# Seven half-size products for eight in the last seven groups of the gate projection, with the scan blocks on a twelve-half grid

## The chip, the cores and the metric

One NeuronCore of one Trainium2 chip runs the whole program. The metric is the device time of one execution in microseconds (us); the time of the kernel before is the median of three executions. TensorE is called PE below, VectorE DVE, ScalarE ACT, GpSimd POOL, and SyncE SP.

## What is computed

One decoder layer is computed for 576 tokens (512 of a prompt and 64 new ones) of width 2048. Cut to what matters here:

```
proj = einsum('bld,dn->bln', x, w_in)               # x: tokens x 2048, w_in: 2048 x 10240
u_a, z_a, b_c, c_c, h_c, z_c, g_a, g_c = split(proj) # widths 6 x 1024, then 2 x 2048
...
h  = associative_scan(lam, B u_a)                    # complex diagonal state, 64 groups of 16 channels
y_a = gelu(Re(C h) + d * u_a); y_a = y_a * sigmoid(y_a @ w_glu)
y_a = (y_a * silu(z_a)) @ w_out_a
y_c = (b_c * conv3(c_c * h_c) * silu(z_c)) @ w_out_c
merged = sigmoid(g_a) * y_a + sigmoid(g_c) * y_c
out = layernorm(2**0.25 * x + merged @ w_o)
```

All of it is in float32. The two gates g_c and g_a, 4096 outputs of width, are where the change is made: a plain product of a 4096 x 2048 weight with the 2048 x 576 tokens, followed by a sigmoid.

## The kernel before

**Halves.** All dense products are cut into halves. A half is one weight tile of 1024 inputs by 128 outputs (512 KB); it is loaded by SP into one of three buffers `w_raw`, and split by ACT into a rounded part `w_hi` and by DVE into the rest `w_lo`, since PE multiplies in a format that keeps only part of a float32. Tokens are split in the same way (`xh`, `xl`). For each of the 8 blocks of 128 inputs PE then does three products (hi with hi, hi with lo, lo with hi), each on two sets of 288 tokens: 48 matmuls of 288 columns in a half. In the last stage, the output projection, tokens are taken 288 at a time, and a half there has 24 matmuls.

**Order.** The program is written out by hand, engine by engine, as a loop over h, the number of the half. Halves 0 to 15 make u, 16 to 79 the four inputs of the convolution, 80 to 95 z_a (`H_ZA`), 96 to 159 the gates (`H_G`), 160 to 167 the GLU (`H_GLU`), then 16 halves for each of the two output products, and 64 short ones for the last. In step h of its loop ACT and DVE make the split of half h + 2 (`split(h + 2)`). ACT's part waits until half h - 1 is done, since buffers go round by three. What takes the accumulators of half h waits for `half_done` of h, so it stands at the end of step h.

**The scan.** It is cut into 8 blocks of 8 groups. Every step of a block has a place in the loop over h: `ssm_step(h, off)` gives b when h = 16 + SSM_PER * b + off. `SSM_PER` is 16. A block takes: loads of its matrices and of u by POOL (`load_mats`, `load_u`), DVE's tables and matrices, at off 7 a first product on PE (`states_in`, with `taps`), DVE's scan, swaps of halves through POOL's DMA queue, at off 19 the second product on PE (`outputs`), and last gelu and a store to `y_dram`. DVE and ACT do these in `scan_steps(h)`, which stands at the end of step h, behind what waits for half h.

**Around the GLU.** The GLU needs y, eight pieces of 128 x 576, read back from `y_dram` into two buffers `y_in`, and split by ACT (`y_high`) and DVE (`yl`). This was done one piece in each of the steps 152 to 159, `Y_LOAD` to `Y_LOAD` + 8. The GLU's steps on ACT and DVE also wait for `sz_in` and `gc_in`, which SP loads once the last sigmoid is stored.

Of the kernel before, what the change touches and what calls it, by code (L numbers as in the profile page):

```python
# [10 lines left out]
P = 128  # L11
# [23 lines left out]
NG = 8  # L35
NW = 3
# [16 lines left out]
H_GLU = H_G + 4 * KX  # L53
# [3 lines left out]
O_PER = 2 * KX  # L57
H_END = H_O + 2 * O_PER


SSM0 = H_CONV
SSM_PER = 16
Y_LOAD = SSM0 + SSM_PER * (BLK - 1) + 23

# [11 lines left out]
def ssm_step(h, off):  # L76

    b, r = divmod(h - off - SSM0, SSM_PER)
    return b if r == 0 and 0 <= b < BLK else None

# [14 lines left out]
def build(nc, d):  # L95
# [80 lines left out]
    st = u_raw  # L176
# [17 lines left out]

    r = Region(s0)
    yh = r("yh", [P, NB, TOK], F32R)
    yl = r("yl", [P, NB, TOK], F32R)
    y_in = [r(f"y_in{i}", [P, TOK]) for i in range(2)]
    r2 = r.at
    merged = r("merged", [P, KX, TOK])  # L200
    r = Region(x0)
    gch = r("gch", [P, NB, TOK], F32R)
    gcl = r("gcl", [P, NB, TOK], F32R)
    gah = r("gah", [P, NB, TOK], F32R)
    gal = r("gal", [P, NB, TOK], F32R)
    assert r.at <= s0
# [7 lines left out]
    mh = nc.alloc_sbuf_tensor_at("mh", [P, KX, TOK], F32R, offset=x0)  # L214
    ml = nc.alloc_sbuf_tensor_at("ml", [P, KX, TOK], F32R, offset=s0)


    r = Region(x0 + 4 * KX * TOK)
    r_all = r("r_all", [P, KX, TOK])
    assert r.at <= s0  # L220
# [155 lines left out]
    norm_ready = sem("norm_ready")  # L376
    out_ready = sem("out_ready")
# [12 lines left out]
    def _(sp):  # L390

        def load_half(h):
            if h >= H_END:
                return
            if h >= NW:
                sp.wait_ge(lo_ready, h - NW + 1)
            sp.dma_start(w_raw[:, h % NW, :], d["w"][h if h < H_O + O_PER else h - O_PER]).then_inc(raw_loaded[h % NW], 16)

# [33 lines left out]
        for h in range(H_CONV, H_GLU):  # L432
# [11 lines left out]
            if Y_LOAD <= h < Y_LOAD + NB:  # L444
                n = h - Y_LOAD
                if n == 0:
                    sp.wait_ge(y_made, BLK)
                    sp.wait_ge(y_stored, U_LOAD * (BLK - 1))
                if n == NB - 1:
                    sp.wait_ge(y_stored, U_LOAD * BLK)  # L450
                if n >= 2:
                    sp.wait_ge(yl_ready, n - 1)
                sp.dma_start(y_in[n % 2][:, :], y_dram[n]).then_inc(y_loaded[n % 2], 16)
        store_out(NB + 2 * KX - 1, g_sig, 2 * KX, sg_dram[2 * KX - 1])
# [24 lines left out]
        for s in range(4):  # L479
            sp.wait_ge(out_stored[s], 16 * (NB + 2 * KX) // 4)  # L480
        for n in range(2):
            load_sz(n)
            load_gc(n)
# [47 lines left out]
    def _(pool):  # L531
# [21 lines left out]
        def load_u(b):  # L553
            for s in range(2):
                pool.wait_ge(u_stored[s], 16 * (b + 2 - s) // 2 if b < NB - 1 else 16 * NB // 2)
            if b:
                pool.wait_ge(hl_ready, b)
# [30 lines left out]
        def scan_moves(h):  # L588
            if (b := ssm_step(h, -1)) is not None:
                load_mats(b)  # L590
            if (b := ssm_step(h, 2)) is not None:
                load_u(b)
# [3 lines left out]
            if (b := ssm_step(h, 12)) is not None:  # L596
                pool.wait_ge(s_ready, b + 1)
                swap(v_sw, v_st, s_swapped)
            if (b := ssm_step(h, 11)) is not None:
                store_k(b)  # L600
            if (b := ssm_step(h, 13)) is not None:
                load_lt(b)
            if (b := ssm_step(h, 25)) is not None:
                store_y(b)

        store_mq()
        for h in range(SSM0 - 1, SSM0 + SSM_PER * (BLK - 1) + 26):
            scan_moves(h)

    @blk.tensor  # L610
    def _(pe):
# [83 lines left out]
        for h in range(H_CONV, H_GLU):  # L695
# [3 lines left out]
            if (b := ssm_step(h, 19)) is not None:  # L699
                outputs(b)  # L700
# [3 lines left out]
            half(h, par, xh, xl, h % 2 * KH, h % 2 == 0, h % 2 == 1)  # L704
        for h in range(H_GLU, H_O):
# [35 lines left out]
        for h in range(H_O, H_END):  # L741
            t, u = divmod(h - H_O, O_PER)
            if u % 4 < 2:
                fresh(h % 2)
# [6 lines left out]
            half(h, h % 2, mh, ml, (u // 2) % 2 * KH, u % 4 < 2, u % 4 >= 2,  # L751
# [4 lines left out]
    def _(act):  # L756

        def split(h):
            if h >= H_END:
                return  # L760
            act.wait_ge(raw_loaded[h % NW], 16 * (h // NW + 1))
            if h >= NW:
                act.wait_ge(half_done, h - NW + 1)
            act.activation(w_hi[h % NW][:, :], w_raw[:, h % NW, :], ACT.Copy).then_inc(hi_ready, 1)  # L764
# [15 lines left out]
        def scan_steps(h):  # L780
            if (b := ssm_step(h, 19)) is not None:
# [5 lines left out]
            if (b := ssm_step(h, 4)) is not None:  # L787
# [5 lines left out]
            if (b := ssm_step(h, 5)) is not None:  # L793
                act.wait_ge(lb_ready, b + 1)
                act.activation(lbh[:, :, :], mb[:, :, :, :].rearrange("p g c s -> p g (c s)"), ACT.Copy)\
                   .then_inc(lbh_ready, 1)
                act.wait_ge(u_loaded, U_LOAD * (b + 1))
# [13 lines left out]
            if (b := ssm_step(h, 10)) is not None:  # L811
# [4 lines left out]
            if (b := ssm_step(h, 15)) is not None:  # L816
# [4 lines left out]
            if (b := ssm_step(h, 22)) is not None:  # L821
# [24 lines left out]
        for h in range(H_CONV, H_ZA):  # L846
            split(h + 2)
            n, l = divmod(h - H_CONV, 8)
# [14 lines left out]
            scan_steps(h)  # L863

        for h in range(H_ZA, H_G):
            split(h + 2)
            if h % 2:
# [5 lines left out]
            scan_steps(h)  # L873
# [5 lines left out]
        for h in range(H_G, H_GLU):  # L879
            split(h + 2)  # L880
            if Y_LOAD < h <= Y_LOAD + NB:
                y_high(h - Y_LOAD - 1)
            if h % 2:
                n = (h - H_G) // 2
                act.wait_ge(half_done, h + 1)
                act.wait_ge(out_stored[n % 4], 16 * ((n + NB) // 4))
# [3 lines left out]
            scan_steps(h)  # L890
# [77 lines left out]
    def _(dve):  # L968
# [6 lines left out]
        def split(h):  # L975
            if h >= H_END:
                return
            dve.wait_ge(hi_ready, h + 1)
            dve.tensor_tensor(w_lo[h % NW][:, :], w_raw[:, h % NW, :], w_hi[h % NW][:, :].bitcast(F32),  # L979
                              ALU.subtract).then_inc(lo_ready, 1)  # L980

# [177 lines left out]
        def turn_table(b):  # L1159
# [452 lines left out]
```

## Time and profile before

| | |
|---|---|
| Median of 3 executions | 1577.58 us (1576.66 to 1577.72) |
| Profiled execution, its own time | 1577.16 us |
| Its span, first to last instruction | 1575.3 us |
| Granted TensorE clock, mean | 0.995 |
| PE busy | 1545.9 us, 98% |
| DVE / ACT / POOL busy | 830.0 / 444.3 / 189.0 us |

The span is what the rows count from. 1.9 us of the execution's time lie outside it. Busy is the union of an engine's instructions; a matmul's recorded length (297 ns) overlaps with the next, so PE's pace is read from starts or from counted pieces of the chain, not from that length.

### The profile page before, as it was taken

The page shows a single profiled execution, that of the slowest core. Times are in us where ns is not written, and L with a number is a line of the kernel's source. Part 1 is how long each engine was busy: PE and PEld are TensorE (multiplying, and loading weights), DVE is VectorE, ACT ScalarE, POOL GpSimd, SP SyncE. Part 2 cuts the span into 40 slices and gives each one's busy share as a digit, 9 for nine tenths or more (in the row PEclk, how much of TensorE's full clock was granted, in tenths as well). Part 3 has the DMA queues.
Part 4 walks back from the last instruction along what each step waited for, and adds up shares of the span by engine and source line. Part 5 has one row for each costly group of instructions (what it writes and reads, how often), then busy time and mean ns, then how long its engine had stood idle before and what let it go on. Part 6 is the DMA issues. An engine that isn't in the chain of part 4 may idle for free.

```text
span 1575.3 us, 26995 instructions
## 1 busy us (share of the span) xinstructions
PE 1545.9 (98%) x11690; PEld 1539.2 (98%) x11690; DVE 830.0 (53%) x1177; ACT 444.3 (28%) x582; POOL 189.0 (12%) x348
## 2 busy tenths in 40 slices
PE   8999999999999999999999999999999999999994
PEld 8999999999999999999999999999999999999994
DVE  5977374464463553643633533223733355666887
ACT  4222222222122122222222222133411122333444
POOL 0110040230311311302204113010000000000000
PEclk9999999999999999999999999999999999999997
DMA  9352362452543543634625535344544443555573
GB/s 304 125 152 91 92 166 79 116 158 75 133 133 94 146 117 122 176 109 132 161 83 165 136 115 147 104 156 150 189 141 134 125 127 125 160 187 183 183 221 107
DMA packets 87447, 221.21 MB, mean 140 GB/s; under 512 B 19744, under 2 KB 28576, under 8 KB 87328
## 3 DMA queue, kind: packets, MB, share of 16 engines
q1 hardware_dynamic: 71456, 188.78, 38.6%
q0 software_dynamic: 15872, 30.70, 8.6%
q8 instruction: 92, 1.51, 0.4%
q14 instruction: 27, 0.22, 0.0%
HBM read 186.55 MB, written 28.16 MB: 136 GB/s over the span
## 4 chain that ended last, share of the span: by engine, by line
PE 94%; DVE 3%; SPq 1%; DMA 1%; issue 1%; ACT 0%; DVEq 0%
PE acc L634 91%; SPq L420 1%; DMA w_raw<-in_w 1%; PE s_ps L656 1%; DVE r_all L1495 0%; PE s_ps L680 0%; PE s_ps L682 0%; DVE w_lo L979 0%; DVE r_all L1494 0%; PE s_ps L657 0%; PE s_ps L681 0%; PE s_ps L679 0%; PE k_ps L666 0%; DVE rstd L1488 0%; DVE r_all L1460 0%
## 5 line engine op out<-in xcount | busy, mean ns | idle before, releaser
L634 PE MATMUL acc<-xh,w_hi 128*128 128x288 f32 x2560 | 550.9, 297 | 3.9 <-DVE xl L987 3.7
L634 PE MATMUL acc<-xh,w_lo 128*128 128x288 f32 x2560 | 549.5, 296 | 0.0
L634 PE MATMUL acc<-xl,w_hi 128*128 128x288 f32 x2560 | 549.2, 296 | 0.0
L979 DVE TENSOR_TENSOR w_lo<-w_raw,w_hi 128x1024 fp32r<-128x1024 f32 x263 | 321.8, 1224 | 406.8 <-ACT w_hi L764 405.1
L764 ACT ACTIVATE w_hi<-w_raw 128x1024 fp32r<-128x1024 f32 x263 | 278.0, 1058 | 597.3 <-PE acc L634 578.2
L634 PEld LDWEIGHTS acc<-xh,w_hi 128*128 128x128 f32 x2560 | 412.9, 189 | 6.4 <-DVE w_lo L997 2.3
L634 PEld LDWEIGHTS acc<-xh,w_lo 128*128 128x128 f32 x2560 | 413.4, 188 | 0.0
L634 PEld LDWEIGHTS acc<-xl,w_hi 128*128 128x128 f32 x2560 | 413.4, 188 | 0.0
L634 PE MATMUL acc<-mh,w_hi 128*128 128x288 f32 x512 | 152.2, 297 | 1.0 <-DVEq L983 0.7
L634 PE MATMUL acc<-ml,w_hi 128*128 128x288 f32 x512 | 151.3, 296 | 0.0
L634 PE MATMUL acc<-mh,w_lo 128*128 128x288 f32 x512 | 151.3, 296 | 0.0
L634 PEld LDWEIGHTS acc<-mh,w_hi 128*128 128x128 f32 x512 | 96.1, 188 | 1.7 <-DVEq L983 0.9
L634 PEld LDWEIGHTS acc<-ml,w_hi 128*128 128x128 f32 x512 | 96.1, 188 | 0.2
L634 PEld LDWEIGHTS acc<-mh,w_lo 128*128 128x128 f32 x512 | 96.1, 188 | 0.0
L887 ACT ACTIVATE out_st<-acc 128x576 f32<-128x576 f32 x32 | 20.9, 654 | 189.6 <-PE acc L634 189.6
L564 POOL DMA_DIRECT2D v_sw<-v_st x32 | 18.3, 577 | 446.4 <-DVE v_st L1204 417.7
L634 PE MATMUL acc<-gcl,w_hi 128*128 128x288 f32 x256 | 55.0, 296 | 0.0
L634 PE MATMUL acc<-gch,w_lo 128*128 128x288 f32 x256 | 55.0, 296 | 0.0
L634 PE MATMUL acc<-gal,w_hi 128*128 128x288 f32 x256 | 55.0, 296 | 0.0
L634 PE MATMUL acc<-gah,w_hi 128*128 128x288 f32 x256 | 55.0, 296 | 0.0
L634 PE MATMUL acc<-gah,w_lo 128*128 128x288 f32 x256 | 54.9, 296 | 0.0
L634 PE MATMUL acc<-gch,w_hi 128*128 128x288 f32 x256 | 54.9, 296 | 0.0
(275 smaller groups left out, 1467.1 us busy)
## 6 DMA issues: line engine op xcount, KB each, us to landing
w_raw<-in_w SPq DMA_DIRECT2D x263, 512.0 KB, 3.8
sg_dram<-out_st SPq DMA_DIRECT2D x32, 288.0 KB, 4.6
v_sw<-v_st POOLq DMA_DIRECT2D x32, 144.0 KB, 3.9
gc_in<-sg_dram SPq DMA_DIRECT2D x16, 288.0 KB, 2.7
sz_in<-sg_dram SPq DMA_DIRECT2D x16, 288.0 KB, 2.7
x_in<-in_xT SPq DMA_DIRECT2D x32, 144.0 KB, 2.2
outT<-o_st SPq DMA_DIRECT2D x32, 144.0 KB, 1.8
mb<-mq_dram POOLq DMA_DIRECT2D x8, 512.0 KB, 6.6
```

Of the source, the lines that this page charges most:

```text
L420: sp.dma_start(k_dram[part, b, :, :, 0:KROW - T * GC].rearrange("x p n -> p x n"), zeros[:, :, :]).then_inc(zeros_stored, 16)
L564: pool.dma_start(to[64 * x:64 * x + 64, :, :], of[64 - 64 * x:128 - 64 * x, :, :]).then_inc(done, 16)
L634: ins = pe.matmul(acc[:, par, t, 0:TH], w, m[:, k0 + k, t * TH:(t + 1) * TH], start=first and k == 0 and n == 0, stop=last and k == KH - 1 ...
L656: pe.matmul(out_of(g), lbh[:, g, :], u, start=True, stop=False)
L764: act.activation(w_hi[h % NW][:, :], w_raw[:, h % NW, :], ACT.Copy).then_inc(hi_ready, 1)
L887: act.activation(two(out_st[n % 4][:, :]), halves_of(acc[:, n % 2]), ACT.Sigmoid).then_inc(g_sig, 1)
L979: dve.tensor_tensor(w_lo[h % NW][:, :], w_raw[:, h % NW, :], w_hi[h % NW][:, :].bitcast(F32), ALU.subtract).then_inc(lo_ready, 1)
```

## The change

Three things are changed together.

1. The last seven of the sixteen groups of four halves in the gates (28 halves) are done as seven products for eight. Such a group is two output tiles (of 128) times two input halves (of 1024): weights A11, A12, A21, A22, and tokens in two input halves and two sets of 288. In Winograd's form of Strassen's scheme seven products of 24 matmuls replace eight. The weights of four of them (S1 to S4) are sums, made by DVE in place (`weight_sums`). The tokens of four of them are sums too (`token_sums`, once, in the eight steps before). DVE adds the products up in pieces of 128 x 288 (`keep`, `out_st`), and ACT applies the sigmoid to the finished tile. The 49 units count as halves 132 to 180, so `H_GLU` is 181.
2. `SSM_PER` is 12. The blocks' steps are moved together (`outputs` from 19 to 16, the scan from 11 to 10, the swaps back from 12 to 11), `load_mats` and `load_u` of the next block come right behind the first swap, the scan's result `st` lies in `v_sw`, no longer in `u_raw`, and `scan_steps(h)` stands directly behind `split(h + 2)` in all stages.
3. The pieces of y are loaded and split in steps 175 to 180, the last six units.

```diff
-SSM_PER = 16
-Y_LOAD = SSM0 + SSM_PER * (BLK - 1) + 23
+SSM_PER = 12
+KINDS = ("A11", "A12", "S2", "S1", "S3", "S4", "A22")
+UNIT_AT = {(kind, n): H_S + 7 * n + i for n in range(NSG) for i, kind in enumerate(KINDS)}
+X_SUMS = H_S - 9
+Y_LOAD = UNIT_AT["A11", NSG - 1]
+Y_STEP = (1, 2, 3, 4, 5, 5, 6, 6)
...
+        def load_y(n):
+            if n < 2:
+                sp.wait_ge(y_stored, U_LOAD * BLK)
+                sp.wait_ge(lo_ready, UNIT_AT["S3", NSG - 2] + 1)
+            else:
+                sp.wait_ge(yl_ready, n - 1)
+            sp.dma_start(y_in[n % 2][:, :], y_dram[n]).then_inc(y_loaded[n % 2], 16)
...
+        def product(h, ps, m):
+            (mh_, ml_), k0, t = m
+            pe.wait_ge(lo_ready, h + 1)
+            for k in range(KH):
...
+                for i, (w, x) in enumerate(((wh, mh_), (wh, ml_), (wl, mh_))):
+                    ins = pe.matmul(ps, w, of_half(x[:, k0 + k, :], t), start=k == 0 and i == 0,
...
+        def weight_sums(h):
+            for kind, of, to in (("S3", "A11", "A21"), ("S2", "S3", "A22"), ("S1", "A21", "A22"), ("S4", "S2", "A12")):
...
+                dve.wait_ge(lo_ready, h + 3)
+                if kind in ("S3", "S2"):
+                    dve.wait_ge(group_loaded[to, n % 2], 16 * (n // 2 + 1))
+                dve.tensor_tensor(raw_of(kind, n), raw_of(of, n), raw_of(to, n), ALU.add).then_inc(weight_sum, 1)
+                dve.wait_ge(weight_sum, sum_count(kind, n))
...
         for h in range(H_CONV, H_ZA):
             split(h + 2)
+            scan_steps(h)
...
-            scan_steps(h)
...
+        for h in range(H_S, H_GLU):
+            split(h + 2)
+            weight_sums(h)
...
+            if kind == "S4":
+                dve.tensor_tensor(of_half(o1, 1), k_f, ps, ALU.add).then_inc(c12_ready, 1)
+            if kind == "A22":
+                dve.tensor_tensor(of_half(o2, 0), k_s, ps, ALU.add).then_inc(c21_ready, 1)
...
+            for i, step in enumerate(Y_STEP):
+                if h == Y_LOAD + step:
+                    dve.wait_ge(yh_ready, i + 1)
+                    dve.tensor_tensor(yl[:, i, :], y_in[i % 2][:, :], yh[:, i, :].bitcast(F32), ALU.subtract)\
+                       .then_inc(yl_ready, 1)
```

On PE the place is half 132, the first of the 49. Before, a half goes over both token sets with each weight:

```order
L634 MATMUL acc<-xh,w_hi 128x288 x2
L634 MATMUL acc<-xl,w_hi 128x288 x2
L634 MATMUL acc<-xh,w_lo 128x288 x2
L634 MATMUL acc<-xh,w_hi 128x288 x2
L634 MATMUL acc<-xl,w_hi 128x288 x2
```

And now (`s_ps` is the scan's accumulator, used here for three of the products):

```order
L747 MATMUL acc<-xl,w_hi 128x288 x2
L747 MATMUL acc<-xh,w_lo 128x288 x2
L827 MATMUL s_ps<-xh,w_hi 128x288
L827 MATMUL s_ps<-xl,w_hi 128x288
L827 MATMUL s_ps<-xh,w_lo 128x288
```

Each weight is now used for one token set, so consecutive matmuls go to one place of the accumulator, where before they went to two in turn.

On DVE the place is the end of the gates, just ahead of the GLU (`yl` are the pieces of y, `gcl` the first of the GLU's own work). Before:

```order
L979 TENSOR_TENSOR w_lo<-w_raw,w_hi 128x1024
L1403 TENSOR_TENSOR yl<-y_in_115,yh 128x576
L979 TENSOR_TENSOR w_lo<-w_raw,w_hi 128x1024
L1403 TENSOR_TENSOR yl<-y_in_116,yh 128x576
L979 TENSOR_TENSOR w_lo<-w_raw,w_hi 128x1024
L1410 TENSOR_TENSOR gcl<-gc_in_125,gch 128x576
```

And now, from the sixth of the last seven units on:

```order
L1174 TENSOR_TENSOR w_lo<-w_raw,w_hi 128x1024
L1669 TENSOR_TENSOR out_st_94<-keep_127,acc 128x288
L1678 TENSOR_TENSOR yl<-y_in_121,yh 128x576
L1678 TENSOR_TENSOR yl<-y_in_122,yh 128x576
L1174 TENSOR_TENSOR w_lo<-w_raw,w_hi 128x1024
L1671 TENSOR_TENSOR out_st_95<-keep_125,acc 128x288
L1678 TENSOR_TENSOR yl<-y_in_121,yh 128x576
L1678 TENSOR_TENSOR yl<-y_in_122,yh 128x576
L1174 TENSOR_TENSOR w_lo<-w_raw,w_hi 128x1024
```

The last four pieces of y stand between and behind the last two sums into `out_st`, two to a unit.

On POOL one block's round of DMAs was, before:

```order
L564 DMA v_sw<-v_st 64x576 x2
L586 DMA y_dram<-y_pre 16x8x72 x8
L568 DMA k_dram<-k_hi 128x2x128
L570 DMA k_dram<-k_lo 128x2x128
L564 DMA v_sw<-v_st 64x576 x2
L580 DMA lth<-k_dram 16x8x128 x8
L580 DMA ltl<-k_dram 16x8x128 x8
L548 DMA mb<-mq_dram 128x1x1024
L549 DMA bc<-in_bC 128x1x1024
L550 DMA c_blk<-in_c_blk 128x256
L551 DMA b_blk<-in_b_blk 128x256
L560 DMA u_raw<-u_dram 16x8x72 x8
```

And now:

```order
L679 DMA v_sw<-v_st 64x576 x2
L663 DMA mb<-mq_dram 128x1x1024
L664 DMA bc<-in_bC 128x1x1024
L665 DMA c_blk<-in_c_blk 128x256
L666 DMA b_blk<-in_b_blk 128x256
L675 DMA u_raw<-u_dram 16x8x72 x8
L683 DMA k_dram<-k_hi 128x2x128
L685 DMA k_dram<-k_lo 128x2x128
L679 DMA v_sw<-v_st 64x576 x2
L695 DMA lth<-k_dram 16x8x128 x8
L695 DMA ltl<-k_dram 16x8x128 x8
L701 DMA y_dram<-y_pre 16x8x72 x8
```

The next block's twelve loads moved ahead of the second swap and of `lth`, and the store of y moved behind them.

## Rows read from the trace of the kernel before

**Rows 1.** The page: busy time, share and instructions of each engine.

```profile
PE 1545.9 (98%) x11690; PEld 1539.2 (98%) x11690; DVE 830.0 (53%) x1177; ACT 444.3 (28%) x582; POOL 189.0 (12%) x348
```

**Rows 2.** The chain in time: start us, us, what.

```profile
923.93 76.99 PE acc L634 x576
1004.45 352.03 PE acc L634 x2640
1356.96 96.00 PE acc L634 x720
```

**Rows 3.** Timeline of PE at three `states_in`: start us, us, what.

```profile
484.34 0.43 PE L634 MATMUL acc<-xh,w_lo 128*128 128x288 f32 x2
485.04 0.31 PE L656 MATMUL s_ps<-u,lbh 128*128 128x144 f32 x1 [0.27 <-issue]
...
593.32 0.43 PE L634 MATMUL acc<-xh,w_lo 128*128 128x288 f32 x2
594.78 0.30 PE L656 MATMUL s_ps<-u,lbh 128*128 128x144 f32 x1 [1.03 <-DVE lbl L1260]
...
703.06 0.43 PE L634 MATMUL acc<-xh,w_lo 128*128 128x288 f32 x2
703.64 0.30 PE L656 MATMUL s_ps<-u,lbh 128*128 128x144 f32 x1 [0.16 <-issue]
```

**Rows 4.** Timeline of DVE ahead of the first of these.

```profile
479.31 1.23 DVE L1254 TENSOR_TENSOR lcl<-lc,lch 128x1024 fp32r<-128x1024 f32 x1
...
481.91 1.22 DVE L979 TENSOR_TENSOR w_lo<-w_raw,w_hi 128x1024 fp32r<-128x1024 f32 x1
483.05 1.22 DVE L1260 TENSOR_TENSOR lbl<-mb,lbh 128x1024 fp32r<-128x1024 f32 x1
484.18 0.75 DVE L1263 TENSOR_TENSOR u<-u_raw,u 128x576 fp32r<-128x576 f32 x1
```

**Rows 5.** Timeline of DVE, three instructions of `turn_table`.

```profile
440.04 1.13 DVE L1167 TENSOR_TENSOR scr<-coarse,fine 128x512 f32<-128x512 f32 x1
441.09 1.12 DVE L1168 TENSOR_TENSOR scr<-coarse,fine 128x512 f32<-128x512 f32 x1
442.24 0.69 DVE L1169 TENSOR_TENSOR cos<-scr,scr 128x512 f32<-128x512 f32 x1
```

**Rows 6.** Groups by line: count | busy us, mean ns | idle before.

```profile
L979 DVE TENSOR_TENSOR w_lo<-w_raw,w_hi 128x1024 fp32r<-128x1024 f32 x263 | 321.8, 1224 | 406.8 <-ACT w_hi L764 405.1
L764 ACT ACTIVATE w_hi<-w_raw 128x1024 fp32r<-128x1024 f32 x263 | 278.0, 1058 | 597.3 <-PE acc L634 578.2 <-DMA w_raw<-in_w 13.1 <-ACT out_st L887 3.3
L1175 DVE TENSOR_TENSOR scr<-mb,bc 128x1024 f32<-128x1024 f32 x8 | 9.8, 1219 | 0.0
L1452 DVE SCALAR_TENSOR_TENSOR r_all<-x_in,acc 128x288 f32<-128x288 f32 x32 | 14.4, 451 | 15.0 <-PE acc L634 15.0
L1403 DVE TENSOR_TENSOR yl<-y_in,yh 128x576 fp32r<-128x576 f32 x8 | 6.0, 752 | 0.0
L877 ACT ACTIVATE yh<-y_in 128x576 fp32r<-128x576 f32 x8 | 5.4, 670 | 0.0
```

**Rows 7.** Timeline of ACT: a split after a wait for PE, and the GLU's start.

```profile
1385.86 1.06 ACT L764 ACTIVATE w_hi<-w_raw 128x1024 fp32r<-128x1024 f32 x1 [0.24 <-PE acc L634]
...
1087.72 0.65 ACT L887 ACTIVATE out_st<-acc 128x576 f32<-128x576 f32 x1 [4.70 <-PE acc L634]
1094.45 0.69 ACT L894 ACTIVATE gch<-gc_in 128x576 fp32r<-128x576 f32 x1 [4.84 <-DMA gc_in<-yc_dram]
```

**Rows 8.** SP's loads of `y_in`, from their source line.

```profile
DMA to landing us min/median/max: 2.8/4.1/5.5
```

**Rows 9.** Timeline of POOL over one block's loads of `lth` and `ltl`.

```profile
526.30 1.35 POOL L564 DMA_DIRECT2D v_sw<-v_st  x2 [3.60 <-DVE v_st L1218]
544.12 0.62 POOL L548 DMA_DIRECT2D mb<-mq_dram  x1
```

**Rows 10.** Window of first block: us, busy of PE, PEld, DVE, ACT, POOL, clock, DMA.

```profile
158.17:267.08 108.91, 108.64 (x835) 108.16 (x833) 57.76 (x73) 25.64 (x36) 19.01 (x34) 1.00 0.40 113
```

More of the change, by code:

```diff
@@ L79, in ssm_step, with unit_of, sum_count, raw_count @@
     return b if r == 0 and 0 <= b < BLK else None
+def unit_of(h):
+    return KINDS[(h - H_S) % 7], (h - H_S) // 7
+SUM_STEP = {"S3": -2, "S2": -1, "S1": 0, "S4": 1}
+def sum_count(kind, n):
+    return sum(1 for k, at in SUM_STEP.items() for v in range(NSG)
+               if 7 * v + at < 7 * n + SUM_STEP[kind]) + 1
+def raw_count(h):
+    return sum(1 for g in range(h % NW, h + 1, NW) if not H_S <= g < H_GLU)
 class Steps:
@@ L376, in build @@
     norm_ready = sem("norm_ready")
+    xs_loaded = [sem(f"xs_loaded{i}") for i in range(2)]
+    xs_sums = sem("xs_sums")
+    xs_high = sem("xs_high")
+    xs_low = sem("xs_low")
+    group_loaded = {(kind, p): sem(f"group_{kind}_{p}") for kind in ("A11", "A12", "A21", "A22") for p in range(2)}
+    weight_sum = sem("weight_sum")
+    s_kept = sem("s_kept")
+    e_ready = sem("e_ready")
+    f_ready = sem("f_ready")
+    g_ready = sem("g_ready")
+    c11_ready = sem("c11_ready")
+    c12_ready = sem("c12_ready")
+    c21_ready = sem("c21_ready")
+    c22_ready = sem("c22_ready")
     out_ready = sem("out_ready")
@@ L889, in _ @@
                 act.sem_inc(acc_free[n % 2], 1)
-            scan_steps(h)
+            if X_SUMS <= h < X_SUMS + KH:
+                j = h - X_SUMS
+                act.wait_ge(y_done, BLK)
+                act.wait_ge(xs_sums, j + 1)
+                for i in range(2):
+                    act.activation(x2h[:, j + i * KH, :], x_st[j % 2][:, i, :], ACT.Copy).then_inc(xs_high, 1)
+        first = 2 * (KX - NSG)
+        for h in range(H_S, H_GLU):
+            split(h + 2)
+            kind, n = unit_of(h)
+            m = first + 2 * n
+            if kind == "A11":
+                act.wait_ge(half_done, h + 1)
+                if n:
+                    act.wait_ge(c21_ready, n)
+                act.activation(keep[0][:, :], s_ps[:, 0, 0:TH], ACT.Copy).then_inc(s_kept, 1)
+            if kind == "S4":
+                act.wait_ge(c11_ready, n + 1)
+                act.wait_ge(c12_ready, n + 1)
+                act.activation(out_st[m % 4][:, :], out_st[m % 4][:, :], ACT.Sigmoid).then_inc(g_sig, 1)
+            if kind == "A22":
+                act.wait_ge(c22_ready, n + 1)
+                act.wait_ge(c21_ready, n + 1)
+                act.activation(out_st[(m + 1) % 4][:, :], out_st[(m + 1) % 4][:, :], ACT.Sigmoid).then_inc(g_sig, 1)
+            for i, step in enumerate(Y_STEP):
+                if h == Y_LOAD + step:
+                    act.wait_ge(half_done, Y_LOAD + 1)
+                    y_high(i)
         def gc_high(n):
@@ L1165, in turn_table @@
             s = [x[:, 0:NG * CP].rearrange("p (g a r) -> p g a r", g=NG, r=T) for x in scr]
[L1166 to L1169 removed]
+            if b:
+                dve.wait_ge(st_ready, b)
+            if part:
+                dve.wait_ge(lc_ready, b + 1)
+            out, a, op = ((cos, (k[0], k[1]), ALU.subtract), (sins, (ks[1], ks[0]), ALU.add))[part]
+            own.mark(dve.tensor_tensor(s[0], a[0], f[0], ALU.mult))
+            link(dve.tensor_tensor(s[1], a[1], f[1], ALU.mult))
+            link(dve.tensor_tensor(grid(out), s[0], s[1], op))
         def input_matrix(b):
```

311 lines of the change are left out of this document (228 added, 83 removed).

## Prediction

> **What bounds the kernel now.** I read the page first. PE is busy for 1545.9 of 1575.3 us and the next engine, DVE, for 830.0 [rows 1]. The chain in order of time then shows whether PE is really paced by its own matmuls: a run of 2640 matmuls takes 352.03 us with nothing between them [rows 2], 0.1333 us each. So a half of 48 takes 6.40 us, and whatever lies beside PE costs nothing until it delays a matmul. The same pace holds for 576 in 76.99 us, and for 720 in 96.00 us in the last stage, where halves have 24 matmuls and take 3.20 us [rows 2].
>
> Where PE waits inside the program, the timeline of PE shows it at `states_in` [rows 3]. The last matmul before it starts at 484.47 (the second of the pair at 484.34), the next at 485.04. One step of 0.13 is normal, so 0.43 us are lost. In the same way 1.19 us are lost at 594.78 and 0.32 at 703.64. In the trace the first of the eight blocks loses nothing, three lose 0.43, one 1.19 and three 0.32: 3.5 us. These, the start and the end are all that PE gives away, so the change is worth what it takes from PE's instructions, less new waits.
>
> **Fewer matmuls.** 28 halves of 48 go (1344), 49 products of 24 come (1176). 168 matmuls less, at 0.1333 us: 22.4 us. This asks that a matmul that writes where the one before wrote keeps its pace. The last stage has that pattern today, and has the pace [rows 2]. **-22.4.**
>
> **The waits at `states_in`.** What is late there today is the low part of u: the instruction that makes it ends at 484.18 + 0.75 = 484.93, and PE starts 0.11 us later [rows 3, 4]. Ahead of it on DVE stand `lcl`, two gelu instructions (the row of the first is left out; together 1.5 us), the split and `lbl` [rows 4]. In the new order the gelu has another step (off 19, not 6), and DVE no longer takes what waits for the end of the half before the scan. ACT's split begins at best 0.26 us into a half, or 1.03 us if a sigmoid or copy of 0.65 [rows 7] stands before it, and DVE's follows when that is done, 1.06 and a hand-over of 0.03 later [rows 5, 6]: at 2.12 at worst. Then `w_lo`, `lcl` and `lbl` follow at 1.14 us each (483.05 - 481.91) and u at 0.75 [rows 4]: done at 6.29, PE ready at 6.40, just when the half ends. Bounds: nothing gained, or all 3.5. I take 3.2, since each step has its row. **-3.2.**
>
> **The groups of seven.** PE takes 7 x 3.20 = 22.4 us for a group. DVE has 7 splits of 1.22, 4 weight sums (nearest row: `tensor_tensor` of 128x1024 in float32, 1.22) and 7 sums of 128x288 (0.45) [rows 6], 16.6 us; ACT 7 of 1.06, two sigmoids of 0.65 [rows 7] and a copy, 9.2 us. Neither is the bound by its sum. But they hand work to each other in order, and the tightest stretch is this: ACT's split of the next group's A11 may start when S3 is done on PE, 16.0 us into the group, and the low part of the next S1 is needed at 22.4 + 9.6 = 32.0. Between lie 0.26 for the start [rows 7], 4 high splits (4.24), 4 low (4.88), the sums for S3, S2 and S1 (3.66), the sums into `out_st` of S4 and A22 (0.90) and their sigmoids (1.30), since each step here waits for the one before: 15.24. Some 14 hand-overs of about 0.03 (442.24 - 441.09 - 1.12) [rows 5] make it 15.7. 0.3 us are left, of which PE's own 0.11 goes. So I expect no real wait, and put 0.5 for all six passages; none at the low end. At the high end hand-overs of 0.1 and small sums that take 0.65 give 17.0, 1.0 us a group, 6 us. **+0.5.**
>
> Here a page speaks. In rows 5 DVE's second instruction starts 1.05 us after the first, which is 1.13 long, and the third, which waits for a semaphore of the second, 1.15 after one of 1.12. A wait on itself costs 0.10 us, and six of them are in the stretch above (counted in it, as full lengths). The Trainium skill, "VectorE: DVE Perf Modes", section "The DRAIN you can't avoid", says that a semaphore between two such instructions "costs nothing extra here"; by it the stretch would be 15.1. The trace does not agree, and the sum goes by the trace.
>
> **The eight steps before them** add to DVE, each, 4 instructions of 0.45 and 2 of 0.75 [rows 6]: 3.3 us beside a split of 1.22 in 6.40. DVE waits there for ACT's high parts, which in odd steps stand behind a sigmoid at the end of the half, so DVE runs some 3.6 us late. A split is made two halves ahead and ends 2.6 us into its half, so 10 us of lateness hide. The first four weight tiles are loaded late (behind the last pair of tokens), 2 to 3 us past their time; same cover. **0**, up to 3 if the loads crowd.
>
> **The pieces of y.** Before, each had a half to itself. Now eight share six units of 3.20 us, with two buffers, so a piece's load can't start before the low part of the piece two before is made. A load takes 2.8 to 5.5 us, 4.1 in the middle [rows 8], the split 0.67 and 0.75 [rows 6]. I follow the last group from its start, at 4.1: the low part of piece 0 at 11.8, which makes DVE's split for S3 0.2 late (13.0 for 12.8), **+0.4** with PE's start; piece 1 at 14.3, piece 2 loaded at 16.0, made at 17.5; then A22's split, two sums and piece 3 at 20.8; piece 5 loaded at 24.9, made at 26.4. Behind it ACT and DVE do the split for half 182, the last sum (28.4) and the sigmoid (29.1), and only then piece 6 (30.6) and 7 (32.0). The GLU's first half starts at 22.65 and needs piece k 0.80 k later: piece 6 at 27.45, so PE waits 3.2, and for piece 7 0.6 more: 3.8. With loads of 2.8 the same walk leaves 1.0. The loads of weights around them are few then, so I take a value between. **+2.5.**
>
> The last sigmoid also ends about 6 us into the GLU, where it ended 0.85 in before; `gch` came 6.1 us behind it [rows 7], then some 6 us of chain to the split of the GLU's fourth half: about 19, needed at 21.7. This is covered, with 2.5 us to spare.
>
> **The twelve-half grid** takes nothing from PE: the same 8 blocks. What could cost is an engine that no longer keeps up. From the first `states_in` to the second DVE is busy for 57.8 of 108.9 us [rows 10], of which 16 splits are 19.5. A block will last 12 halves and its own 6.1 us on PE (108.9 less 16 times 6.40 and the wait of 0.43), some 83 us. If all of DVE's other 38.3 us stay, and the earlier block's gelu and y sums (3 us) come on top, that is 56 with 12 splits: two thirds. A step of the scan may end a half late on DVE without a cost, by the 10 us above. **0.**
>
> **Sum**, against the profiled execution's 1577.16: -22.4 -3.2 +0.5 +0.4 +2.5 = -22.2, **1555.0 us**. That execution is 0.4 under the median 1577.58, which is nothing here.
>
> **Rivals.** *The groups are paced by DVE and ACT.* For it: 0.3 us of slack in a stretch of 16. Against: the rows add up to less. At 1 to 3 us a group over six or seven, 1561 to 1575. Chance 0.12.
>
> *POOL's queue paces the scan (ends on the slower side).* A block has 42 DMAs there, and `lth` now stands behind twelve loads of the next block, which the order shows. At today's pace, 18 DMAs from 526.30 to 544.12 [rows 9], 0.99 us each, a round takes 42 of some 83 us; the first swap can go 4.1 us into off 8, the twelve loads are issued by 5 us into off 10, and `ltl` is issued about the end of off 13 and landed some 5 us into off 14, over a half before `outputs` at off 16, 8 us early. To lose what is gained, each of 8 `outputs` must wait 2.8 us, so POOL must be 11 us later over those 30 DMAs: 1.35 us each in place of 0.99. From there on the change is slower: at 1.6, 18 us late, 10 us a block, 1635 us. Idle for "issue" in the same bursts is up to 3 us at a time, so a crowded queue is possible. Chance 0.04.
>
> *The change doesn't do what it says, or gives it back*: the pause at the GLU lets TensorE's clock fall, or the y chain loads at 5.5 us and repeats. A few us more, 1560 to 1566 within the first case's upper end; matmuls at a slower pace in `s_ps`, no gain, 1577. Chance 0.03.
>
> **The numbers.** Forecast as above 0.81, its own range from all low ends (no wait in the groups, 1.0 for y, all 3.5 back: 1552) to 6 for the groups, 3.8 for y and 1 at the entry (1563). The range 1551.5 to 1563 leaves out about 2 in 10. Within 0.2% (3 us), about what a measurement of this kernel can tell from no change, I put 0.02; slower 0.04; faster 0.94.
>
> **What would show it.** Right: some 168 fewer matmuls, products of 3.20 us through the seven groups, `states_in` at most 0.1 us behind, and one gap of 1 to 4 us in the first half of the GLU before the seventh block. Wrong: gaps of PE before the matmuls of S1 or S3 in each group (released by `w_lo`); PE idle before `outputs` released by `lth`; a granted clock below 1.00 behind the GLU's gap.

## The result, and the profile after

The changed kernel takes 1561.04 us in the median of four executions (1557.92 to 1562.55), the kernel before 1577.65 us on the same chip (1576.66 to 1578.08): a ratio of 0.9892, 95% interval [0.9879, 0.9904]. That is 16.6 us faster, 6 us less than forecast and inside the range. The profiled execution took 1557.92 us, the fastest of the four, with a span of 1556.1. Of the runs below, one execution of grid (5157 us) and two of all4 (2401 and 2990 us) took far longer than every other; they are left out of all medians and ratios, and no trace shows why.

The page, busy time of each engine (answers to rows 1):

```profile
PE 1524.7 (98%) x11522; PEld 1518.4 (98%) x11522; DVE 935.0 (60%) x1323; ACT 475.9 (31%) x626; POOL 187.5 (12%) x348
```

PE has 168 matmuls fewer and is still busy for 98%. DVE went from 830.0 to 935.0 us, which nothing on PE feels by itself. The timeline of PE at one `states_in` (answers to rows 3: start us, us, what):

```profile
489.36 0.43 PE L747 MATMUL acc<-xh,w_lo 128*128 128x288 f32 x2
489.63 0.23 PE L769 MATMUL s_ps<-u,lbh 128*128 128x144 f32 x1
```

And DVE ahead of it (answers to rows 4):

```profile
484.58 1.23 DVE L1174 TENSOR_TENSOR w_lo<-w_raw,w_hi 128x1024 fp32r<-128x1024 f32 x1 [0.40 <-ACT w_hi L926]
485.72 1.22 DVE L1471 TENSOR_TENSOR lcl<-lc,lch 128x1024 fp32r<-128x1024 f32 x1
486.86 1.22 DVE L1477 TENSOR_TENSOR lbl<-mb,lbh 128x1024 fp32r<-128x1024 f32 x1
487.99 0.75 DVE L1480 TENSOR_TENSOR u<-u_raw,u 128x576 fp32r<-128x576 f32 x1
```

The low part of u ends at 488.74, 0.89 us before PE wants it, and PE goes on in step. All eight `states_in` are so: the whole 3.5 us came back.

What PE gives away now stands in the chain in order of time (answers to rows 2):

```profile
1064.14 0.70 ACT out_st L1080
1064.85 5.74 DMA sg_dram<-out_st
1071.11 3.06 DMA gc_in<-yc_dram
1074.25 0.68 ACT gch L1088
1074.93 0.55 ACT sig_t L1099
1075.56 38.66 PE acc L747 x288
1114.23 2.58 issue
1116.80 206.57 PE acc L747 x1536
1323.39 0.77 DVE sz_in L1717
1324.26 13.05 PE acc L747 x96
```

Read it from the top: the last sigmoid of the gates, the landing of its store, the load of `gc_in` that SP issues behind it, `gch`, and only then the sigmoid that frees PE's accumulator. From pitch to pitch PE loses 1.22 us at 1075.56 (third half of the GLU), 2.74 at 1116.80 (`H_OUTC`) and 1.07 at 1324.26 (`H_O`). Behind the second comes one cost more, seen in windows (us, busy of PE, PEld, DVE, ACT, POOL, clock, DMA):

```profile
1116.00:1118.00 2.00, 1.20 (x9) 1.23 (x10) 1.97 (x4) 0.00 (x0) 0.00 (x0) 1.00 0.11 29
1118.00:1121.30 3.30, 3.30 (x16) 3.30 (x16) 2.32 (x4) 1.63 (x2) 0.00 (x0) 0.52 0.96 327
1121.30:1124.00 2.70, 2.70 (x22) 2.70 (x21) 0.58 (x1) 0.00 (x0) 0.00 (x0) 0.95 0.63 198
```

The granted clock is 0.52 for 3.3 us, the lower level of 1.2 GHz, and 13 matmuls have a pitch of 0.240 us for 0.133: 1.4 us. So 1577.2 - 22.4 - 3.5 + 1.2 + 2.7 + 1.1 + 1.4 = 1557.7, against 1557.92 measured. That closes this execution. It leaves open why the other three took 1559.9 to 1562.6; no trace of them was kept, and the experiments show what such executions can lose.

### The profile page after: what moved, and what is told of

Same layout as the page of the kernel before. It is cut to its first block and busy times, and to the rows that moved or that the text cites. A ratio compares the mean times of both kernels' runs of the same rounds, so it can differ in the third digit from the quotient of the medians.

```text
span 1556.1 us, 27026 instructions
## 1 busy us (share of the span) xinstructions
PE 1524.7 (98%) x11522; PEld 1518.4 (98%) x11522; DVE 935.0 (60%) x1323; ACT 475.9 (31%) x626; POOL 187.5 (12%) x348
## 5 line engine op out<-in xcount | busy, mean ns | idle before, releaser
L1174 DVE TENSOR_TENSOR w_lo<-w_raw,w_hi 128x1024 fp32r<-128x1024 f32 x251 | 307.1, 1224 | 307.1 <-ACT w_hi L926 304.1
L747 PE MATMUL acc<-xh,w_hi 128*128 128x288 f32 x2112 | 455.0, 297 | 3.8 <-DVE xl L1194 3.5
L747 PE MATMUL acc<-xh,w_lo 128*128 128x288 f32 x2112 | 453.2, 296 | 0.0
L747 PE MATMUL acc<-xl,w_hi 128*128 128x288 f32 x2112 | 453.1, 296 | 0.0
L926 ACT ACTIVATE w_hi<-w_raw 128x1024 fp32r<-128x1024 f32 x251 | 264.6, 1055 | 565.5 <-PE acc L747 537.6
L747 PEld LDWEIGHTS acc<-xh,w_hi 128*128 128x128 f32 x2112 | 340.6, 189 | 6.1 <-DVE w_lo L1204 2.2
L747 PEld LDWEIGHTS acc<-xh,w_lo 128*128 128x128 f32 x2112 | 341.0, 188 | 0.0
L747 PEld LDWEIGHTS acc<-xl,w_hi 128*128 128x128 f32 x2112 | 341.0, 188 | 0.0
L1174 DVE TENSOR_TENSOR w_lo<-s_raw,w_hi 128x1024 fp32r<-128x1024 f32 x33 | 40.4, 1223 | 17.4 <-ACT w_hi L926 17.2
```

The source lines that it names most:

```text
L747: ins = pe.matmul(acc[:, par, t, 0:TH], w, m[:, k0 + k, t * TH:(t + 1) * TH], start=first and k == 0 and n == 0, stop=last and k == KH - 1 ...
L926: act.activation(w_hi[h % NW][:, :], raw, ACT.Copy).then_inc(hi_ready, 1)
L1174: dve.tensor_tensor(w_lo[h % NW][:, :], raw, w_hi[h % NW][:, :].bitcast(F32), ALU.subtract).then_inc(lo_ready, 1)
```

## The experiments

The sums of waits below are read from the pitch of PE's matmuls, less the normal step; the matmuls at a slow pace are summed in the same way (2.3 us of these are in every trace, before included). Kernels of one batch ran on one chip, beside executions of the kernel before: the first four (again to slack) beside a median of 1577.69 us, the next four (upool to all4) beside 1577.43, the last three beside 1578.09. A ratio of a run is to this median of its own batch, with its 95% interval.

**again.** The changed kernel, not edited.

> The changed kernel as it is, once more. Its four times so far lie 4.6 us apart (1557.92 to 1562.55), those of before 1.4. Theory A (the loss lies at the start of the GLU, in a load of gc_in and sz_in that waits for the store of the last sigmoid, and varies with how long that store takes): a new profile has its waits of PE at the same places, the GLU's third half, the start of the first output product and the start of the last stage, but with other lengths, 5 to 10 us in all; the rest of the span agrees within 0.3 us. Theory B (the spread is the clock's or the machine's, spread over the program): the same waits with the same lengths, and the difference somewhere else.

Measured: 1567.18 us in the median of six (1563.38 to 1571.59), ratio 0.9931 [0.9916, 0.9947]. The interval doesn't meet the first one, 0.9879 to 0.9904, though it is the same program. The profile (1566.35 us) says why, in its waits of PE (waited for: us in total, times, longest us):

```profile
PE s_ps L792 <- DMA ltl<-k_dram: 3.8, 3, 1.5
...
PE acc L747 <- issue: 2.6, 1, 2.6
...
PE acc L747 <- ACTq L1101: 1.3, 1, 1.3
```

The first row is not in the first profile at all. `outputs` waited for the landing of `ltl` in three of eight blocks (1.42, 1.20 and 1.68 us from pitch to pitch), and matmuls at a slow pace came to 7.0 us. Neither theory had this: the loss is at a new place, not at the start of the GLU. In the first profile `lth` and `ltl` had landed 3.3 to 4.7 us before `outputs` in seven blocks; in the kernel before it was 17 to 23. The last block has 9.9. The change had used up most of this cover, and whether the rest was enough differed from one execution to the next. One program can thus come out 6 us apart in two batches, so small differences between batches are judged by the waits in the traces below.

**early.** SP loads `sz` and `gc` ahead of the last two stores of `sg`.

```diff
+            if h == H_GLU - 1:
...
+                for m in range(2):
+                    load_sz(m)
+                    load_gc(m)
             if kind == "A12" and n or h == H_GLU - 1:
```

> One edit: gc_in and sz_in of the first two pieces are loaded ahead of the last two stores of sigmoids, and wait only for what they read and overwrite. Theory A: the waits of PE in the GLU and at the first output product go (1.2 and 2.7 us in the profile of the changed kernel), and with them the stretch at half clock behind the second (about 1.4 us): 1552.5 to 1553.5 in the best case and a spread under 1.5 us, so 5 to 8 us under the changed kernel's median. The 1.1 us at the start of the last stage stay. Rival C (ACT and DVE are late into the GLU because the last four pieces of y stand in the way): gch can't start before about 5 us into the GLU whatever is loaded, and the waits shrink by a third at most, 1 to 2 us.

Measured: 1558.47 us (1557.46 to 1564.17), ratio 0.9874 [0.986, 0.9889]. No wait in the GLU, 1.30 us in place of 2.74 at `H_OUTC`, 1.07 at `H_O` as ever. The profiled execution is the slowest of the four and lost 3.69 us at two `outputs` besides. The median is 8.7 us under that of again, the run beside it. But the best execution is 4 us above the 1553.5 that was expected at most, and the four lie 6.7 us apart, not 1.5. So the wait for the stores was real, and it isn't what makes the executions differ. That half of the theory was wrong.

**grid.** The kernel before with the twelve-half grid and its moved steps alone, on every engine.

> The kernel before with the twelve-half grid alone: blocks every twelve halves, steps directly behind the splits, loads moved, no products of seven. The pieces of y stay in steps 152 to 159. If the waits at states_in were all that this part gives: 1577.6 less 3.3 to 3.5, 1574.1 to 1574.4. If the earlier end of the scan does something else for the time (less traffic late in the program), more than that. If POOL's queue costs something, PE idles before outputs and less than 3 us are gained.

Measured: 1579.31 us in the median of eleven, ratio 1.0011 [1.0002, 1.002]. The waits at `states_in` were gone, and in the profile 2.56 us at two `outputs` stood in their place. A further 1.8 us were lost ahead of the first `states_in`, where the granted clock was 0.50 from 11.5 to 18.2 us; only upool's trace has the like, so this is not counted against the edit. So this half of the change gave nothing in these executions.

**slack.** The low part of S1 is made twice, one DVE instruction more in the tightest place of each group.

```diff
+            if H_S <= h < H_GLU and unit_of(h)[0] == "S1":
+                link(dve.tensor_tensor(w_lo[h % NW][:, :], raw, w_hi[h % NW][:, :].bitcast(F32), ALU.subtract))
```

> The changed kernel, with the low part of the weight S1 made twice in each of the seven groups (the same value written twice, 1.25 us more of DVE at the tightest place). Predicted slack there: 0.3 us, less PE's own 0.1. If that stretch of hand-overs is what a group can bear, PE waits in six of seven groups for about 1.0 us each, before S1 or S3 or both: 5.5 to 7.5 us over the changed kernel. If a group has more cover than that (DVE is busy 16.6 of 22.4 us), nothing or under 1 us.

Measured: 1573.86 us in the median of ten (1569.71 to 1582.36), ratio 0.9975 [0.996, 0.999]. DVE and PE in one group of its profile:

```profile
1034.53 1.22 DVE L1175 TENSOR_TENSOR w_lo<-s_raw,w_hi 128x1024 fp32r<-128x1024 f32 x1 [1.20 <-ACT w_hi L926]
1035.79 1.22 DVE L1176 TENSOR_TENSOR w_lo<-s_raw,w_hi 128x1024 fp32r<-128x1024 f32 x1
```

```profile
1035.89 0.29 PE L827 MATMUL s_ps<-x2h,w_lo 128*128 128x288 f32 x1
1037.16 0.37 PE L827 MATMUL acc<-x2h,w_hi 128*128 128x288 f32 x1 [0.98 <-DVE w_lo L1176]
```

DVE's instruction adds 1.26 us, and PE's step grows from 0.13 to 1.27, by 1.14. So the cover was 0.12 us, and six of seven groups pay. That is 6.8 us, and the median is 6.7 over that of again, the run beside it, as forecast. It also prices a wait of DVE on itself: 1.26 from start to start here, 1.14 where none stands between two such instructions (484.58 and 485.72 above).

**upool.** The kernel after with one change: POOL issues the eight loads of u for the next block behind `load_lt`, no longer between the two swaps.

```diff
             if (b := ssm_step(h, -3)) is not None:
                 load_mats(b)
-                load_u(b)
...
                 load_lt(b)
+            if (b := ssm_step(h, 0)) is not None:
+                load_u(b)
+            if (b := ssm_step(h, 25)) is not None:
+                store_y(b)
```

> The kernel after with one change on POOL's queue: the eight loads of u for the next block are issued behind load_lt (step 12) and no longer between the two swaps (step 9). Theory (POOL's queue feeds the scan too late): in the first profile of the kernel after, the scan of block 3 ended at 435.70 us, and the second swap was issued only at 440.62 us, behind u_raw loads that cost 7.9 and 2.4 us of waiting in the queue; without them lth and ltl land 8 us or more before outputs instead of 0.3 to 4.7, none of the eight outputs waits over 0.3 us, and the spells of matmuls at a pitch of 0.240 us behind those waits are gone. Times: 1556 to 1559 us, median 1558, executions within 3 us. Rival (the landing is late because of the DMA engines, whatever the order): outputs still waits 1.2 to 2.4 us in one to three blocks, median as the kernel after, 1561 to 1567 us, with a spread of 5 to 8 us.

Measured: 1558.72 us (1556.64 to 1559.8), ratio 0.9877 [0.9864, 0.989]. POOL's timeline for block 2, first of the run steps (below), which has the order of the changed kernel:

```profile
343.79 0.56 POOL L678 DMA_DIRECT2D u_raw<-u_dram  x1 [2.18 <-issue]
352.16 3.16 POOL L678 DMA_DIRECT2D u_raw<-u_dram  x6 [7.81 <-issue]
359.23 0.53 POOL L678 DMA_DIRECT2D u_raw<-u_dram  x1 [3.91 <-issue]
359.75 0.74 POOL L686 DMA_DIRECT2D k_dram<-k_hi  x1
360.49 0.74 POOL L688 DMA_DIRECT2D k_dram<-k_lo  x1
361.22 1.27 POOL L682 DMA_DIRECT2D v_sw<-v_st  x2
...
381.99 1.05 POOL L698 DMA_DIRECT2D ltl<-k_dram  x2 [4.24 <-issue]
```

and of upool:

```profile
352.54 0.74 POOL L683 DMA_DIRECT2D k_dram<-k_hi  x1 [10.09 <-issue]
...
354.88 1.07 POOL L679 DMA_DIRECT2D v_sw<-v_st  x2 [0.87 <-DVE v_st L1432]
...
369.75 1.05 POOL L695 DMA_DIRECT2D ltl<-k_dram  x2 [2.69 <-issue]
```

In the first the scan's result was there at 353.76 and the swap that takes it went out at 361.22; the queue held POOL up for 2.2, 7.8 and 3.9 us in the loads of u. In the second the swap waits for DVE alone. The last `ltl` goes out 12 us earlier, and lands 11.5 us before `outputs` (8.7 to 11.5 in seven blocks, 4.1 in one). No `outputs` waits. The median is at the upper side of what was expected, since a new 0.5 us at one `states_in` and the start's own variation are in it. By its interval the median is no better than that of the changed kernel in the first comparison, and is better than again's; that the wait is gone and the executions lie within 3.2 us of each other is the finding. All the traces together bear it out. In the six with u loaded where the changed kernel has it (the changed kernel, again, early, grid, slack, steps), `ltl` came too late in 10 of 48 blocks; in the six with the new order (upool, gridpool, all4, all4n5, upnarrow, upparity) in none of 48. The cover is not back everywhere: in four of these six traces one block has only 3.7 to 4.4 us.

**gridpool.** The run grid with the same order on POOL.

> The kernel before with the twelve-half grid of the scan alone (as the run grid, 1579.9 us), and with the loads of u behind load_lt. Theory (POOL's queue took back what the grid gave): the 3.5 us of waits at states_in are gone and no wait at outputs comes in their place: 1577.65 - 3.4 = 1574.2 us (1573 to 1575.5). Rival (the grid gives nothing for another reason, such as the clock): 1577 to 1580 us, as grid.

Measured: 1573.49 us in the median of seven (1572.89 to 1574.87), ratio 0.9976 [0.9965, 0.9986]: 3.9 us under before, where grid was 1.6 over. Behind the first 40 us its profile has no wait of PE at all at a scan step. So where POOL loads u decides whether the grid's gain is kept. The two runs stood on different chips, but each beside the kernel before, and their intervals are apart.

**steps.** early, with the first half at `H_OUTC` waiting for `gcl` block by block, and the last stage taking the other accumulator first. POOL's order is that of the changed kernel.

```diff
-                half(h, h % 2, gch, gcl, 0, True, True)
+                half(h, h % 2, gch, gcl, 0, True, True, gc_there if h == H_OUTC else None)
...
-                fresh(u % 2)
+                fresh((u + 1) % 2)
```

> The kernel after with three changes in the last third, the scan's order unchanged: sz and gc loaded ahead of the last two stores of sg (as the run early), the matmuls of the first half at H_OUTC wait block by block for gcl instead of for all eight, and the halves of the last stage take the other accumulator first. Theory: the run early left 1.30 us at H_OUTC and 1.07 us at H_O, and both go; the waits at outputs stay as they fall (0 to 4 us with their clock spells). Profile: no wait of PE over 0.5 us behind 1065 us. Times: 1553 to 1562 us, median 1557. Rival (the wait at H_OUTC moves into the blocks, since the GLU's chain runs at 5.85 us a step): 1 us or more of waits inside the first half at H_OUTC, gain of parity alone 1.1 us, median 1558.

Measured: 1557.55 us (1555.56 to 1562.14), ratio 0.9875 [0.9862, 0.9888]. Behind 1065 us only 0.56 and 0.18 are left, for pieces of y (under 0.5 was expected), and the block-by-block wait for `gcl` costs nothing, so the rival is out. The profiled execution (1562.14) shows what one late landing costs. PE:

```profile
383.90 0.43 PE L750 MATMUL acc<-xh,w_lo 128*128 128x288 f32 x2
386.29 0.31 PE L798 MATMUL s_ps<-u,lth 128*128 128x144 f32 x1 [1.96 <-DMA ltl<-k_dram]
...
388.00 0.41 PE L800 MATMUL s_ps<-h,lch 128*128 128x144 f32 x1
...
391.84 0.78 PE L750 MATMUL acc<-xh,w_hi 128*128 128x288 f32 x2
392.41 0.68 PE L750 MATMUL acc<-xl,w_hi 128*128 128x288 f32 x2
```

and the same windows as above, of this stretch:

```profile
388.00:391.00 3.00, 3.00 (x16) 3.00 (x15) 1.29 (x2) 0.00 (x0) 0.53 (x1) 0.50 0.44 49
391.80:394.60 2.80, 2.80 (x14) 2.80 (x14) 0.00 (x0) 0.05 (x1) 0.00 (x0) 0.51 0.58 227
```

The wait is 2.12 us. From 387.8 to 394.6 the clock is at its lower level, and the pitch of the scan's matmuls is 0.213 us for 0.112. The two spells of this trace cost 3.2 us each (8.7 of slow matmuls in all, less the common 2.3), so a spell costs more than the wait before it.

**all4.** steps and upool together, four edits to the kernel after.

> The run steps with the loads of u behind load_lt as well. Theory: both sets of waits gone: from the profiled execution of the kernel after (1557.92 us, no wait at outputs) less 1.22, 2.74, 1.4 of a clock spell and 1.07 us: 1551.5 us; with 0.3 us for what is left, 1551 to 1553 us, executions within 2 us of each other. Rival (waits at outputs come from the DMA engines and not from the order on POOL's queue): as steps, 1553 to 1562 us with the same spread.

Measured: 1552.04 us in the median of four (1551.21 to 1552.15), ratio 0.9835 [0.9821, 0.9849]. It is the fastest of all kernels here, 5.5 us under steps on the same chip, and these four lie within 1 us. Its profiled span is 1550.2 us, 10.2 less than that of steps: 3.5 of waits at `outputs`, 6.4 of slow matmuls behind them, and 0.3 ahead of the first `states_in`.

**all4n5.** all4 with `NSG = 5`, five groups of seven.

> The run all4 (1552.1 us) with five groups of seven products instead of seven (NSG = 5). Theory (a group saves its 24 matmuls and costs nothing beside): two groups fewer are 48 matmuls of 0.1333 us more, 1552.1 + 6.4 = 1558.5 us (1558 to 1559.2). Rival (the groups cost something that the count of matmuls hides, such as the 0.1 to 0.3 us in the last one, in each of them): less than 6.4 us, down to 5.5 us: 1557.6 us.

Measured: 1559.82 us (1559.41 to 1560.31), ratio 0.9885 [0.9868, 0.9901]; the span is 1557.6, 7.4 over all4. The matmuls explain 6.4. Another 0.8 is in the GLU's first half, where the pieces of y now come later:

```profile
PE acc L751 <- DVE yl L1683: 1.6, 1, 1.6
```

against, in all4:

```profile
PE acc L751 <- DVE yl L1683: 0.5, 1, 0.5
```

The groups themselves can be timed from the first matmul of the first to the first of the GLU: 157.04 us for the 49 products of all4, 112.24 for the 35 of all4n5. At 3.20 each that is 0.24 us over the count in both. So what a group saves is its 24 matmuls. The rival for this run is out, and the result lies above the range given for it because of the pieces of y and of a chip that is 0.7 us slower for the kernel before too.

**upnarrow.** upool, with `sz` and `gc` loaded when the stores of `sz` have landed, and no longer all those of `sg`; SP's order is unchanged.

> The run upool (1558.7 us) with one wait moved: sz and gc are loaded once the stores of sz have landed, no longer all the stores of sg. Theory (gch was 6 us late because the last store of sg took 5.8 us to land): the first loads are issued within 1 us of that store's issue, the wait in the third half of the GLU (1.40 us in upool) is gone and the one at H_OUTC falls from 2.73 us to under 0.6 us or to nothing, with its spell of slow matmuls: 1558.7 - 1.4 - 2.2 - 1.4 = 1553.7 us (1553 to 1555). Rival (the load is late because the sigmoid ahead of the last store is, 2.7 us into the GLU): half of the waits stay, 1556 to 1557 us.

Measured: 1555.83 us (1554.24 to 1558.2), ratio 0.986 [0.9845, 0.9874]. SP now issues the loads right behind the last store:

```profile
1063.51 2.04 SPq L518 DMA_DIRECT2D sg_dram<-out_st  x2
1065.80 0.32 SPq L578 DMA_DIRECT2D sz_in<-sz_dram  x1
```

The wait in the GLU's third half, 1.40 us in upool, is gone; 0.20 us is left in the first, for a piece of y. The one at `H_OUTC` falls from 2.73 to 1.40, and the granted clock stays at 1.00 behind it. So 2.5 of 4.1 us of waits went with the wait for the stores. The time lies between the theory and the rival, but the rival's reason, the place of the last sigmoid, isn't what holds `gch` up now. ACT is idle before it, for the load:

```profile
1072.09 0.69 ACT L1091 ACTIVATE gch<-gc_in 128x576 fp32r<-128x576 f32 x1 [4.44 <-DMA gc_in<-yc_dram]
```

That load was issued at 1066.17 and landed 5.83 us later, where in the changed kernel it took 3.06. In early it was issued at 1074.14, ahead of the last stores and 2.3 us into the GLU, and took 7.78. The DMA engines are fuller while it is on its way, with a busy share of 0.94 in early and 0.95 in upnarrow, for 0.76 in the changed kernel (windows, as above; early, upnarrow, the changed kernel):

```profile
1074.10:1081.90 7.80, 7.80 (x59) 7.61 (x58) 3.12 (x5) 2.90 (x4) 0.00 (x0) 1.00 0.94 300
1066.00:1072.00 6.00, 5.96 (x44) 5.64 (x43) 2.56 (x3) 1.64 (x2) 0.00 (x0) 1.00 0.95 355
1071.00:1074.00 3.00, 3.00 (x25) 3.00 (x24) 0.00 (x0) 0.00 (x0) 0.00 (x0) 1.00 0.76 240
```

So an earlier issue bought a slower landing, and the 1.30 us of early and the 1.40 here stand behind that. That the traffic is the cause is argued and not shown: no run changed it alone.

**upparity.** upool with the accumulators of the last stage exchanged.

> The run upool (1558.7 us), with the halves of the last stage taking the other accumulator first. Theory (the 1.07 us at H_O are the wait for the accumulator that the half right before it used): that wait is gone, 1557.6 us (1556.5 to 1558.5). Rival (the wait is for merged, mh and ml): a wait of about 1 us stays at H_O and the time is upool's.

Measured: 1557.64 us (1556.84 to 1558.25), ratio 0.987 [0.9855, 0.9884]. The 1.07 us at `H_O` is gone. In the time alone the 1.1 us to upool is within the intervals; the trace decides. The reason is a parity: `H_O` is 221 now and was 200, so its first half took the accumulator that half 220 had just filled.

## Why the prediction came out as it did

**Fewer matmuls, -22.4: right.** 168 are gone, and every product of the first six groups lasts 3.20 us. all4n5 gives 6.4 us for two groups by the count, and matmuls that write where the last one wrote kept their pace.

**The waits at `states_in`, -3.2: right in place, 3.5 measured, but it was given back.** The low part of u is there 0.9 us early. What the sum lacked is that the same regrouping moved the late thing to `outputs`. The time of grid shows none of the gain, that of gridpool has it.

**Groups of seven, +0.5: right.** The margin from the low part of S1 to its product was 0.26 to 0.28 us in six groups, where PE's own start takes 0.11 and the walk had said 0.3. Only the last group, with the pieces of y in it, loses 0.13 and 0.10. slack shows how near that is: one instruction there, and six of seven groups pay. A wait on itself costs DVE 0.12 us here (1.26 less 1.14), beside the 0.10 of rows 5. The Trainium skill, "VectorE: DVE Perf Modes", section "The DRAIN you can't avoid", has it cost nothing extra in a measurement of eight copies in a row; for the `tensor_tensor` instructions of this kernel the traces don't agree.

**The pieces of y, +0.4 and +2.5: the second was mis-sized.** No piece was waited for longer than 0.15 us in the first profile, and in four others (again, steps, all4, upnarrow) PE waited 0.2 to 0.8 us for one. The error was the load time: I chose between 2.8 and 5.5 us, but said that there is little other traffic then. SP's loads of `y_in` in the kernel after:

```profile
DMA to landing us min/median/max: 2.7/2.8/3.1
```

The walk with loads of 2.8 had left 1.0. A range from rows under heavier traffic should not have been averaged in.

**"This is covered, with 2.5 us to spare": the step that failed in the last third.** The last sigmoid ended 3.4 us into the GLU, earlier than the 6 forecast. Yet `gch` came 12.9 us in, where I had 12. Its store took 5.7 us to land, where before it took 2.1, and `gc_in` is loaded only behind that. The walk then asked only when the fourth half's split would be late. It left out two things. The sigmoid that frees the accumulator of the GLU's first half stands right behind `gch` on ACT, and the third half wants it 12.8 us in, at 1074.2: 1.22 us. And the GLU's chain makes a step in some 5.85 us to a half's 6.40, so a lateness at its start is worked off by 0.55 us a half and is still there at `H_OUTC`, eight halves on, where PE asks for all of `gcl` at once. The wait of 2.74 us, and the slow spell that it sets off, come from that. early and upnarrow take a part of it away, and steps, which asks for `gcl` block by block, the rest.

**Parity at `H_O`, +1.07: not in the sum.** I had counted the halves and not asked which accumulator each takes.

**The rival "POOL's queue paces the scan" happened in part, and it is the larger lesson.** I had put `ltl` 8 us early at 0.99 us a DMA. It was 3.3 to 4.7 early in the good case. In the bad one PE stood waiting and began 0.25 after the landing, in one to three of eight blocks. The price was not the long steady wait that I had worked out. It was 1.2 to 2.4 us at times, and with the clock behind it up to 5.5. The slack of 8 us came from a mean; rows 9 span 18 DMAs, and the queue's stops inside such a stretch (7.8 us at once above) fall in single places of the order. The place mattered: the twelve loads had been behind `lth`, and eight of them now stood ahead of the swap that the scan waits for.

So the likely account of the median, 1561.04: the profiled 1557.9, and 2 to 5 us from `outputs` that are late in some executions. It isn't shown for these four, of which only the fastest has a trace. 0.81 for the forecast with no such wait was too sure. That the range held was partly luck: its upper end had been put there for other costs, in the groups and for y, that did not come. The profiled execution is only 2.9 us over the forecast for a like reason: 2.5 us for y that were not paid stand against 6.4 us that were not in the sum (1.2 + 2.7 + 1.4 + 1.1).

**What stays open.** Why one store takes 5.7 us to land and another 2.1 wasn't tried. The traces show how full the DMA engines were from issue to landing, for the last store of the changed kernel (5.7 us), of the kernel before (2.1) and of again (6.7):

```profile
1064.80:1070.60 5.80, 5.80 (x44) 5.68 (x43) 2.71 (x3) 2.24 (x4) 0.00 (x0) 1.00 0.61 191
1088.40:1090.50 2.10, 2.10 (x18) 2.10 (x17) 0.86 (x1) 1.06 (x1) 0.00 (x0) 1.00 0.36 140
1072.40:1079.10 6.70, 6.07 (x45) 5.75 (x44) 2.74 (x3) 2.19 (x3) 0.00 (x0) 1.00 0.46 165
```

Before, the store went out alone; now it goes with another store, a weight tile and two pieces of y. But the longest landing has the middle share, so the share alone doesn't order them. Nor was it tried why the batch of again had more late blocks than the first profile: the traces show when the queue stops, not why it stops there.

## What to carry to other kernels

When steps move closer together, list for each transfer how long before its use it lands, before and after; a cover that shrinks from 20 us to 4 is a cost that one profile can hide, so look at the spread of the executions as well as at their median. On a queue that one engine feeds in order, put the load that is needed last behind the transfers that a chain waits for, even if it is ready sooner. And follow a late start of a chain to the next place where an engine asks for all its results at once: with 0.55 us regained a half it arrives there nearly whole.

## What the runs showed of the hardware that was not expected

A wait of TensorE can cost more than its length. Behind waits of 1.91, 2.12, 2.37 and 2.73 to 2.83 us (the last five times) the granted clock fell to its lower level every time. Behind 1.32, 1.37 and 1.68 us it did in three traces; behind 1.19 to 1.42 us in eleven other places, and behind 1.72 us in one, there was no such spell. In nine of the eleven spells the fall came 0.6 to 2.5 us after the matmuls had begun again (386.29 and 387.7 above). In the other two it came while PE still waited. These are again, whose matmuls begin at 1125.47, and slack, at 1089.60 (windows, as above):

```profile
1124.95:1125.40 0.45, 0.00 (x0) 0.00 (x0) 0.45 (x2) 0.00 (x0) 0.00 (x0) 0.50 0.00 0
1089.00:1089.50 0.50, 0.00 (x0) 0.00 (x0) 0.50 (x1) 0.50 (x1) 0.00 (x0) 0.50 0.95 230
```

A spell cost 3.1 to 3.3 us behind `outputs` in each of six cases, 1.3 to 1.6 behind the wait at `H_OUTC`, and 2.8 in the GLU.

GpSimd issues a DMA in 0.53 us, but inside a series of eight DMAs, with no wait of the program between them, it then stops for up to 8.5 us at once (the loads of `u_raw` in the changed kernel: seven stops of 7.1 to 8.5 us; those of `lth` 3.7 to 5.9), with no release that the profile shows ("issue"). So the order of the DMAs decides whom such a stop hits.

The first load of `gc_in`, 288 KB, took 3.1 us to land at a DMA busy share of 0.76, and 5.8 and 7.8 us at 0.95 and 0.94, where it was issued earlier, among other transfers. `gch` came 2.7 us earlier into the GLU for a load issued some 7 us earlier (early).
